# Hybrid encoder step: attention weights turned six tiles behind their scores, not five

## The reference

```python
def stick_breaking_block(q_blk, q_pos, k, v, k_pos):
    z = jnp.einsum("bqhd,bkhd->bhqk", q_blk.astype(jnp.float32), k.astype(jnp.float32)) * SB_SCALE
    mask = k_pos[None, :] < q_pos[:, None]
    log_1mb = jnp.where(mask, jax.nn.log_sigmoid(-z), 0.0)
    log_a = jax.nn.log_sigmoid(z) + lax.cumsum(log_1mb, axis=3, reverse=True) - log_1mb
    a = jnp.where(mask, jnp.exp(log_a), 0.0)
    return jnp.einsum("bhqk,bkhd->bqhd", a, v.astype(jnp.float32))
```

## Time and profile before

| | |
|---|---|
| median of three runs | 2583.7 us (2583.33 to 2584.07) |
| the profiled execution's own time | 2587.18 us |
| its span, first to last instruction | 2585.5 us |
| mean granted TensorE clock | 0.979 |
| busy: PE, PEld, DVE, ACT, POOL | 94%, 52%, 55%, 39%, 35% |

### The profile page before, as it was taken

One profiled execution on the slowest core, in us unless ns is written; L12 is line 12 of the kernel. 1 busy time (PEld: TensorE's weight loads), 2 busy tenths in 40 slices (PEclk: granted clock), 3 DMA queues, 4 the chain that ended last, 5 costly groups with the idle time before them and its releaser, 6 DMA issues.

```text
span 2585.5 us, 36302 instructions
## 1 busy us (share of the span) xinstructions
PE 2431.2 (94%) x14328; PEld 1349.6 (52%) x14328; DVE 1415.9 (55%) x1861; ACT 1018.5 (39%) x1555; POOL 892.8 (35%) x1061
## 2 busy tenths in 40 slices
PE   4899899899998889999999999899999999999998
PEld 3445455444444444454565665345666544688733
DVE  4747665488888887889655554415333302433214
ACT  1522233499999895324443442102222200133200
POOL 1300000277777773333556556501111250111100
PEclk8899999899999999999999999999999999999999
DMA  7315868332332112222556566654454445476555
GB/s 249 100 50 171 283 235 272 120 99 82 99 84 81 34 66 93 78 94 84 165 179 212 179 198 234 227 196 155 155 163 131 139 138 180 153 224 203 186 164 167
DMA packets 216387, 395.63 MB, mean 153 GB/s; under 512 B 30189, under 2 KB 152365, under 8 KB 207642
## 3 DMA queue, kind: packets, MB, share of 16 engines
q1 hardware_dynamic: 199226, 331.45, 40.1%
q10 hardware_dynamic: 16992, 61.87, 7.7%
HBM read 302.97 MB, written 90.30 MB: 152 GB/s over the span
## 4 chain that ended last, share of the span: by engine, by line
PE 58%; DVE 9%; ACT 4%; POOL 4%; DMA 3%; issue 3%; SPq 0%; POOLq 0%; DVEq 0%; ACTq 0%
PE ps L2457 20%; PE ps L2497 15%; PE ps L2426 12%; PE ps L2361 3%; DMA dn_dram<-work 3%; DVE work L1709 3%; PE ps L2236 2%; POOL work L880 2%; PE ps L2213 2%; PE ps L2252 2%; ACT ps L1188 2%; ACT work L1176 2%; DVE work L1866 1%; DVE work L1706 1%; DVE work L1456 1%
## 5 line engine op out<-in xcount | busy, mean ns | idle before, releaser
L2457 PE MATMUL ps<-hidden_t,work 128*128 128x384 f16 (+1 forms) x3696 | 515.2, 303 | 1.9 <-ACT work L1307 1.1
L2497 PE MATMUL ps<-work 128*128 128x512 f16 x2244 | 472.5, 380 | 8.5 <-DVE work L1964 5.9
L2457 PEld LDWEIGHTS ps<-hidden_t,work 128*128 128x128 f16 x3696 | 361.4, 98 | 155.7 <-ACT work L1307 1.7
L2120 PE MATMUL ps<-hidden_t,work 128*128 128x416 f16 x1920 | 353.6, 345 | 14.2 <-DVE hidden_t L1474 10.0
L2426 PE MATMUL ps<-hidden_t,work 128*128 128x384 f16 x2112 | 347.6, 328 | 4.1 <-DVE work L1921 4.1
L2497 PEld LDWEIGHTS ps<-work 128*128 128x128 f16 x2244 | 206.4, 98 | 274.0 <-issue 29.8
L880 POOL TENSOR_TENSOR work<-work 128x512 f32<-128x512 f32 (+2 forms) x320 | 306.8, 965 | 112.4 <-DVE work L1709 63.9
L2426 PEld LDWEIGHTS ps<-hidden_t,work 128*128 128x128 f16 x2112 | 207.5, 98 | 144.3 <-issue 9.6
L2120 PEld LDWEIGHTS ps<-hidden_t,work 128*128 128x128 f16 x1920 | 190.3, 99 | 164.8 <-issue 17.8
L1709 DVE TENSOR_TENSOR_SCAN work<-ps,work 128x512 f32<-128x512 f32 x192 | 237.4, 1270 | 35.2 <-ACT ps L1188 34.3
L841 POOL TENSOR_TENSOR work<-work,col 128x1 f32<-128x1 f32 x68 | 33.2, 488 | 586.2 <-DVE work L1459 586.2
(11 more groups left out here) (243 smaller groups left out, 2723.5 us busy)
## 6 DMA issues: line engine op xcount, KB each, us to landing
work<-dn_dram ACTq DMA_DIRECT2D x96, 512.0 KB, 3.6
work<-gs_dram SPq DMA_DIRECT2D x88, 512.0 KB, 4.2
work<-gs_dram SPq DMA_DIRECT2D x44, 768.0 KB, 4.3
work<-in_w_ada SPq DMA_DIRECT2D x24, 1024.0 KB, 5.7
work<-in_w_gu SPq DMA_DIRECT2D x46, 512.0 KB, 7.1
work<-in_w_gu SPq DMA_DIRECT2D x22, 1024.0 KB, 5.9
gs_dram<-work SPq DMA_DIRECT2D x22, 1024.0 KB, 5.7
gs_dram<-work SPq DMA_DIRECT2D x66, 256.0 KB, 2.4
```

The lines of the kernel that those rows point to most:

```text
L2120: mm = pe.matmul(ps[:, blk, 0:PB], B_HL[s][:, wh * KD * P + k * P:wh * KD * P + (k + 1) * P], hidden_t[:, k, xh, PB * blk:PB * (blk + 1)], ...
L2457: mm = pe.matmul(ps[:, bank, 0:n], E_GS[j % 2][:, GS_AT[q], wh, k, :], hidden_t[:, k0 + k, xh, at:at + n], start=(q in (1, 2, 5) and k == ...
L2497: mm = pe.matmul(ps[r:r + rows, 2 * slot + half, :], E_HID[:, j, xh, at:at + rows], E_DHL[slab_home(g)][:, wh, 512 * half:512 * (half + 1) ...
```

## The change

Turns, copies, weighing and head results each happen one step later against the scores; the scores, plus, minus, scan and product stay where they are. Since `weigh` does two tiles at a time, and must begin with an even one, it moves from even steps to odd ones. The conditions `m % 4` of the copies move along, so that the same tiles are copied by the same engines. At the end of the stage the loop is one step longer, and the first seven `first_mix` are in it in place of six.

```diff
 POOL
-            for m in range(NTILE + 12):
+            for m in range(NTILE + 13):
                 if m < NTILE:
                     product(m)
-                if m >= 11 and ends_block(m - 11):
+                if m >= 12 and ends_block(m - 12):
                     head_split(blk, min(m + 1, NTILE))
                     blk += 1
...
 ACT
-            for m in range(NTILE + 9):
+            for m in range(NTILE + 10):
                 if m % 2 == 0 and m + 2 < NTILE:
                     plus(m + 2)
                 if m % 2 == 1 and m + 1 < NTILE:
                     minus(m + 1)
-                if 5 <= m < NTILE + 5 and m % 4 != 2:
-                    at_copy(m - 5)
-                if m >= 8 and ends_block(m - 8):
-                    head_low(blk, m - 8)
+                if 6 <= m < NTILE + 6 and m % 4 != 3:
+                    at_copy(m - 6)
+                if m >= 9 and ends_block(m - 9):
+                    head_low(blk, m - 9)
                     blk += 1
...
 DVE
-            for m in range(NTILE + 10):
+            for m in range(NTILE + 11):
...
-                if 6 <= m < NTILE + 6 and m % 4 == 3:
-                    at_copy(m - 6)
-                if m >= 9 and ends_block(m - 9):
+                if 7 <= m < NTILE + 7 and m % 4 == 0:
+                    at_copy(m - 7)
+                if m >= 10 and ends_block(m - 10):
                     head_out(blk)
                     blk += 1
...
 PE
-            for m in range(NTILE + 7):
+            for m in range(NTILE + 8):
                 if m + 3 < NTILE:
                     scores(m + 3)
-                if m == 5:
+                if m == 6:
                     pe.wait_ge(kvt_out, 40)
                     pe.wait_ge(mix_set, 1)
-                if 5 <= m < NTILE + 5:
-                    turn_weights(m - 5)
-                if m >= 8 and m % 2 == 0:
+                if 6 <= m < NTILE + 6:
+                    turn_weights(m - 6)
+                if m >= 9 and m % 2:
+                    weigh(m - 9)
                     weigh(m - 8)
-                    weigh(m - 7)
                 if m >= NTILE + 1:
                     first_mix(m - NTILE - 1)
-            first_mix(6)
             first_mix(7)
```

## The result

The changed kernel takes **2618.7 us** (median of 4 runs, 2618.1 to 2619.3) against 2583.9 for the kernel before in the same job: a ratio of 1.013, 95% interval 1.0118 to 1.0141. That is 34.8 us slower, where 18.4 were forecast. The profiled execution's span is 2617.2 us against 2585.5, so 31.7 more; the other 3.1 us of the 34.8 are there because the profiled execution of the kernel before happened to lie 3.3 us above its median, and that of the changed kernel 0.2 above.

The account below looks back on a forecast made before the run. ACT's order was taken as the bound before, the second pair's lengthened loop after; 18.0 us for eight heads, less 1.0 at the start, plus 1.4 at the drain, gave 2583.7 + 18.4 = 2602.1 us, range 2581 to 2616.

Parts of the forecast that it names:

- signs named beforehand: Changed profile: ACT busy 57 to 59 us of a 65 us head, plus waiting 80 or more, copies' waits nearly gone.
- faster rival: Attention stage: ACT stays the bound and loses gaps and half its turn waits, together 22 us, giving 2562; chance 0.13.
- sum for a head: Attention stage: ten units of the second pair's loop, corrected for diagonals and head_low, 65.1 against 62.85 us, 18.0 for eight heads.
- each pair's loop: Dependence from one unit's minus through scan, scores and plus to the next: 6.88 us first pair, 6.65 second pair.
- coupling to the second: First pair's loop leads only from one full unit to the next; 0.05 us a head, bounds 0 and 1.5.
- the walk: Adding operation times and hand-overs around the two pairs' dependence loops in the attention stage, giving 6.88 and 6.65 us.
- four diagonal units: First pair's loop in a head: each diagonal unit takes 2.0 us off, lowering 68.8 to 60.8 us.
- second pair's chain: Tiles 2 and 3 of a unit: loop grows from 5.85 to 6.65 us, longer than ACT's 6.02, and leads.
- profiled execution's offset: Whole program: the median of the runs lies 3.5 us below the profiled execution, so 2605.6 becomes 2602.1.
- rival called slower still: Attention stage: the two loops feed one another and w_ada falls between scan and completing scores; 29 us, 2613; chance 0.12.
- ACT's order sets the pace: Kernel before, attention stage: a full unit takes ACT's own 6.02 us, with the waits for turns on top.
- Start and drain: Ends of the attention stage: gain of 1.0 us at PE's first turn, loss of 1.4 behind DVE's copy of tile 313.

Follow-up runs that it names:

- e_odd_first: e_even_low with only the weighing of kt 0 and 1 moved to the odd step, between a first pair's scores; ratio 1.0099, stage 528.1 us.
- e_odd_second: e_even_low with only the weighing of kt 2 and 3 moved to the odd step, between a second pair's scores; ratio 1.0111, stage 529.7 us.
- e_fold: The changed kernel with the two small matmuls L2227 moved behind the unit's first turn; ratio 1.012, stage 529.3 us.
- e_low_late: The changed kernel with head_low, head_out and head_split one more step later, so head_low is behind minus; ratio 1.0117, stage 526.2 us.
- e_three: The changed kernel with L2227 behind the first turn, head results one more step later, DVE's copy ahead of the unit's first scan; ratio 1.0082, stage 520.8 us.
- e_even_low: The kernel before with head results, turns and ACT's copies a step later, weighing and DVE's copy unmoved; ratio 0.9987, stage 500.2 us.
- e_half_ada: The changed kernel without the last four of the eight matmuls of the w_ada product (L2211); ratio 1.013, stage 530.8 us.
- e_single: e_low_late with one weighing at each step instead of a pair at each odd one; ratio 1.0318, stage 578.4 us.

## Why the prediction was wrong in size

**The direction and its cause held.** The weigh pairs between opening and completing scores cost 28.7 us with all else equal, of the 30.0 by which the stage grew; the other parts are small and of both signs. Most of the signs named beforehand are there: copies wait 5.9 us, turns but for the first no longer wait for POOL, ACT is busy for 57 to 59 us of a head, completing scores start where the weigh pair ends. Plus waits 74.2 us, a little short of the 80 or more foretold. From one full unit's minus to the next, where 6.6 to 6.9 was foretold, the head that begins at 553 us has 6.94, 6.95 and 6.58 for first pairs and 7.54, 7.50 and 6.28 for second ones (L2227 and head_low fall into the two long steps), so all lie outside, three of them by less than 0.1. The faster rival (ACT stays the bound, 2562) fell: ACT's copies lost 26.7 us of waiting and plus gained 65.8.

**The step that failed is the sum for a head**, 65.1 us. It walked each pair's loop by itself, took the first pair's as slack ("gives less ... 60.8") and its coupling to the second as 0.05 with a bound of 1.5. A head measures 66.3 or 67.3, mean 66.8 in heads 1 to 4, against 61.7 or 63.9, mean 62.8, before: 4.0 more in place of 2.25; over all eight it is 30.0 / 8 = 3.75. The runs show in its place:
- The first pair's chain is not slack but close behind the second's. Its steps between full units are 6.94, 6.96 and 6.83 us (means over heads 1 to 4), where the walk had 6.88. But the 8.0 us that I took off a head for its four diagonal units, an estimate by the columns, isn't there: a head is 66.8, only 2.0 below 68.8. What a narrow unit saves in its own loop seems to be taken up by the other chain. And e_odd_first, with a weigh pair in the first pair's gap only, has a stage 27.9 us over its base, where the walk had nothing.
- The second pair's chain leads, but it too is longer than 65.1. In e_odd_second, with its weigh pair alone and DVE's copy out of the way, a head is 66.5. Left out of it was L2227, 0.36 us two or three times a head (1.8 us of the stage by e_fold).
- head_low, put in at 2.5 us a head or 20 for the stage, gives 4.9 when it is moved away (e_low_late). That term was larger than the whole 18.0: without it the walk has 62.55 us a head, no longer than before. The kernel without all three small terms (e_three) should by the walk have lost nothing, and its stage is 19.7 us longer. So the forecast came as near as it did by luck: head_low was some 15 us too large, the rest some 27 too small.

Of the 16.4 us by which the time was missed (34.8 against 18.4) the stage is 12.0, the rest of the program 1.3, and 3.1 come from the profiled execution's offset, which was taken as the same 3.5 us for both kernels. That two chains cross, each lengthening the other, is argued from e_odd_first's timeline and from the small terms; no run prices it by itself.

The rival called slower still, with 66.5 us a head and 29 us for the stage, came nearest (30.0 measured). Its first half, that the loops feed one another, fits the runs above. Its second half, the w_ada product between scan and scores, is not borne out: half of L2211 gone changed the stage by 0.3 us.

**The base was read too simply.** "ACT's order sets the pace" at 6.02 a full unit was wrong as an account of the kernel before: moving POOL's split alone gave 11.9 us, and half a weigh pair 5.9, with ACT's order untouched. And 6.02 was the shortest step between full units in its head: by the same timelines of ACT the others are 6.35 and 6.50, and in the next head 6.10, 6.72 and 6.74. A chain over POOL, PE, DVE and ACT paced it. Whether that spoiled the difference isn't shown; POOL is not on the changed kernel's chain.

**Start and drain.** PE's first turn still waits for POOL, but less (the kernel before: 2.12):

```profile
496.85 1.08 PE L2236 MATMUL ps<-ident,work 128*128 128x128 f32 x4 [0.88 <-POOL work L880]
```

It starts 0.85 us earlier, of which 0.4 is the stage's own earlier start; 1.0 was the forecast. It bought nothing: the first head, that wait included, is 68.05 us against 66.5. What follows the last of these minus is 2.0 us longer in the profiled executions, where 1.4 was the forecast for the drain. But the same stretch varies by 7 us among the kernels here (1594.2 in e_even_low, 1601.1 in e_half_ada), so this term is neither shown nor refuted.

The range, up to 2616, was too narrow above: it went to the slower rival's 2613 and hardly beyond, where that rival had no room for its own uncertainty.

**What stays open.** In the changed kernel moving head_low behind minus helps (4.9 us), in the kernel before the head results a step later are 6.6 us worse than the split later alone (495.8 against 489.2); whether that is head_low or head_out was not tried. A version that keeps the later split and also gains on the turns was not found: e_even_low has its waits of turns and copies down, and is faster than before by only 0.13%.

## What to carry to other kernels

In a hand-written software pipeline, moving an operation to the other parity changes what it stands in front of, and an in-order engine hands every delay to all that is queued behind it: draw the chain through the whole order of the engine, over both halves of the rhythm, and not one loop for each half. Before pricing, read the chain of waits cut to one or two periods; ACT was busy for 94% of a stretch here, and its plus and minus, two thirds of its work in a full unit, held only 17% of that chain. An agreement of the sum is no test of its terms: here one that was too large covered others that were too small. Then test a change of many parts by kernels that differ by one part each, in both directions, for the part that pays may be hidden under the part that costs.

## What was unexpected of the hardware

Two f32 matmul calls of 64 output partitions each, to the lower and the upper half of the PSUM partitions, take 1.01 us back to back, and one of them alone 1.00. PE's busy time shows it too. The group of the changed kernel and then that of e_single, with the same 640 matmuls:

```profile
L2252 PE MATMUL ps<-work 128*64 128x512 f32 (+3 forms) x640 | 159.9, 555 | 0.0
```

```profile
L2252 PE MATMUL ps<-work 128*64 128x512 f32 (+3 forms) x640 | 300.6, 551 | 0.0
```

The mean of one is the same and the busy time is nearly double. The Trainium skill, page "TensorE: Matmul & The Clock Gate", section "Measured speedup vs the span model", gives a measured gain of 2.38 for three narrow matmuls of 32 columns placed in different column groups. The trace agrees in kind: 1.01 us for two here, against 1.00 for one, is a gain of 2.0. It also means that the comparison in the prediction (four matmuls of 216 ns against 1.01 us) set the sum of four against two that ran beside two. A call of two matmul records takes 1.00 us alone, so some 0.5 us a record, and that 0.86 came near 1.01 bears out neither figure.
